# Linear-attention decays computed in another order, and index scores rectified inside PSUM in groups of four

## What is computed

```python
# gla_mixer: chunks of 64 tokens, 4 heads of 256 features
G = jnp.cumsum(g, axis=2)                       # per chunk, in log space
G_last = G[:, :, -1:]
q_t = q * (GLA_DK ** -0.5) * jnp.exp(G)         # decay of the queries
k_t = k * jnp.exp(-G)                           # growth of the keys
k_s = k * jnp.exp(G_last - G)
...                                             # exp(G_last): decay of a whole chunk

# dsa_mixer: 8 index heads of 64, scores of a query against all earlier keys
rel = jax.nn.relu(jnp.einsum('bthd,bsd->bths', qi_b, ki))
score = jnp.einsum('bths,bth->bts', rel, wi_b) * INDEX_SCALE
score = jnp.where(causal[None], score, -jnp.inf)
_, idx = lax.top_k(score, topk)                 # 128 keys for each query
...                                             # softmax attention over those keys
```

## Time and profile before

| | us |
|---|---|
| median of 3 runs | 1694.35 |
| lowest, highest | 1693.36, 1698.34 |
| the profiled execution | 1694.79 |
| its span in the profile | 1693.1 |

### The profile page before, as it was taken

How to read it: one execution, slowest core, us unless ns; L and a number is a source line. 1 busy time by engine, 2 the same in 40 slices (tenths; PEclk the granted TensorE clock), 3 DMA queues, 4 the chain that set the end, 5 groups by cost and what they waited for, 6 DMA issues and landing times. The chain is left out here.

```text
span 1693.1 us, 23540 instructions
## 1 busy us (share of the span) xinstructions
PE 1570.6 (93%) x9993; PEld 1332.1 (79%) x9993; DVE 706.2 (42%) x1357; ACT 526.6 (31%) x849; POOL 590.9 (35%) x245
## 2 busy tenths in 40 slices
PE   6998999999999997999999999999999986957998
PEld 5896885998988974687887997999798763557997
DVE  4031440222162546695555117232242346578524
ACT  2354124333122323234444122352322234331210
POOL 5324320333432256444553242333334460512021
PEclk8999999999999997999999999999999987568999
DMA  5223220134322322122111422342222100020111
GB/s 153 76 75 94 69 62 25 52 99 160 107 95 75 88 85 64 33 93 62 38 51 51 162 76 75 112 146 63 83 92 78 48 1 1 0 75 1 51 51 50
DMA packets 115970, 121.60 MB, mean 72 GB/s; under 512 B 14623, under 2 KB 109833, under 8 KB 115610
## 3 DMA queue, kind: packets, MB, share of 16 engines
q1 hardware_dynamic: 112320, 114.16, 21.3%
q10 hardware_dynamic: 3546, 5.94, 1.0%
HBM read 113.80 MB, written 6.29 MB: 71 GB/s over the span
## 5 line engine op out<-in xcount | busy, mean ns | idle before, releaser
L193 POOL TENSOR_TENSOR w_low<-w_ring,w_high 128x2048 fp32r<-128x2048 f32 (+1 forms) x92 | 419.4, 4559 | 853.0 <-ACT w_high L184 852.9
L209 PE MATMUL ps<-w_high,xT_high 128*128 128x256 f32 (+1 forms) x1056 | 304.5, 288 | 7.8 <-POOL w_low L193 3.4
L209 PE MATMUL ps<-w_high,xT_low 128*128 128x256 f32 (+1 forms) x1056 | 298.9, 283 | 0.0
L209 PE MATMUL ps<-w_low,xT_high 128*128 128x256 f32 (+1 forms) x1056 | 298.8, 283 | 0.0
L184 ACT ACTIVATE w_high<-w_ring 128x2048 fp32r<-128x2048 f32 (+1 forms) x92 | 173.5, 1887 | 355.6 <-PE ps L209 342.2
L209 PE MATMUL ps<-xT_high,w_high 128*128 128x512 f32 (+3 forms) x624 | 253.6, 406 | 8.7 <-DVE mix_a L742 7.7
L209 PE MATMUL ps<-xT_low,w_high 128*128 128x512 f32 (+3 forms) x624 | 249.2, 399 | 0.0
L209 PE MATMUL ps<-xT_high,w_low 128*128 128x512 f32 (+3 forms) x624 | 248.5, 398 | 0.0
L209 PEld LDWEIGHTS ps<-w_high,xT_high 128*128 128x128 f32 x1056 | 202.6, 192 | 15.8 <-issue 10.7
L209 PEld LDWEIGHTS ps<-w_low,xT_high 128*128 128x128 f32 x1056 | 202.6, 192 | 1.7 <-issue 1.7
L209 PEld LDWEIGHTS ps<-w_high,xT_low 128*128 128x128 f32 x1056 | 202.1, 191 | 0.0
(11 more groups left out here) (510 smaller groups left out, 2419.5 us busy)
## 6 DMA issues: line engine op xcount, KB each, us to landing
w_ring<-in_gla_w_in_dram SPq DMA_DIRECT2D x24, 1024.0 KB, 5.4
w_ring<-in_dsa_w_in_dram SPq DMA_DIRECT2D x19, 1024.0 KB, 5.2
w_ring<-in_w_in_dram SPq DMA_DIRECT2D x18, 1024.0 KB, 5.2
w_ring<-in_gla_w_out_dram SPq DMA_DIRECT2D x8, 1024.0 KB, 4.9
w_ring<-in_ple_gate_w_dram SPq DMA_DIRECT2D x8, 1024.0 KB, 5.1
w_ring<-in_dsa_w_out_dram SPq DMA_DIRECT2D x8, 1024.0 KB, 5.3
x_scratch<-x SPq DMA_DIRECT2D x4, 1024.0 KB, 6.6
w_ring<-in_w_out_dram SPq DMA_DIRECT2D x4, 768.0 KB, 4.7
```

The source lines that it names most:

```text
L193: self.nc.gpsimd.tensor_tensor(self.slot(self.w_low, i % RING, k, cols), self.slot(self.w_ring, n % RING, k, cols), self.slot(self.w_high, ...
L209: return self.nc.tensor.matmul(out, lhs, rhs, start=first, stop=last, skip_group_check=not check)
```

## The change

In GLA, ACT's one loop over f becomes three: first the eight small chunk decays, then the eight decays of the queries, then the eight growths of the keys, with the two weight copies before f = 0 and f = 4 of the third loop. The semaphore `decays` becomes three, and DVE waits for the chunk decays before L734, for `q_decay` of tile n before its L742, and for `k_growth` of tile f before its L776.

In DSA, ACT rectifies in place: it reads and writes the PSUM bank, and the buffer `relu` in SBUF is gone. The scores take four banks, m % 4. PE waits for DVE's sum four pairs back; ACT waits for PE only. A projection follows after every fourth pair, six in all (n = 4 to 9), so that ten instead of twelve are left between the scores and the logits.

```diff
                 for f in range(NF):
-                    if f >= 4 and f % 2 == 0:
-                        g.split_high(act, c_q + f // 2 + 1)
                     act.wait_ge(sem["decay_log"], past["decay_log"] + f + 1)
-                    nc.scalar.activation(qT[:, f, :], decay_log[:, f, :], ACT.Exp, scale=1.0 / GATE_NORM).then_inc(sem["decays"], add("decays", 1))
-                    nc.scalar.activation(kT[:, f, :], decay_log[:, f, :], ACT.Exp, scale=-1.0 / GATE_NORM).then_inc(sem["decays"], add("decays", 1))
                     ends = decay_log[:, f, :].rearrange("p (c i) -> p c i", i=C)[:, :, C - 1]
-                    nc.scalar.activation(chunk_decay[:, f, :], ends, ACT.Exp, scale=1.0 / GATE_NORM).then_inc(sem["decays"], add("decays", 1))
+                    nc.scalar.activation(chunk_decay[:, f, :], ends, ACT.Exp, scale=1.0 / GATE_NORM).then_inc(sem["chunk_decay"], add("chunk_decay", 1))
+                for f in range(NF):
+                    nc.scalar.activation(qT[:, f, :], decay_log[:, f, :], ACT.Exp, scale=1.0 / GATE_NORM).then_inc(sem["q_decay"], add("q_decay", 1))
+                for f in range(NF):
+                    if f % 4 == 0:
+                        g.split_high(act, c_q + f // 4 + 3)
+                    nc.scalar.activation(kT[:, f, :], decay_log[:, f, :], ACT.Exp, scale=-1.0 / GATE_NORM).then_inc(sem["k_growth"], add("k_growth", 1))
...
-                dve.wait_ge(sem["decays"], past["decays"] + 3 * NF)
+                dve.wait_ge(sem["chunk_decay"], past["chunk_decay"] + NF)
...
                     dve.wait_ge(sem["qk_ready"], past["qk_ready"] + n + 1)
+                    dve.wait_ge(sem["q_decay"], past["q_decay"] + n + 1)
...
                     dve.wait_ge(sem["qk_ready"], past["qk_ready"] + n + 1)
+                    dve.wait_ge(sem["k_growth"], past["k_growth"] + f + 1)
...
-        relu = probT[:, 0:2]
+        score_bank = lambda m: m % 4
...
-        n_scores = DSA_HEADS // 2
+        n_group = 4
+        n_scores = n_group + 3 * IDX_HEADS // n_group
...
-                    if m >= 2:
-                        pe.wait_ge(sem["relu"], past["relu"] + m - 1)
+                    if m >= 4:
+                        pe.wait_ge(sem["summed"], past["summed"] + m - 3)
...
-                    g.product(ps[:, m % 2, 0:n], qiT[rows, h // 2, j * P:(j + 1) * P], kiT[rows, 0:n]).then_inc(sem["index_ready"], add("index_ready", 1))
-                    if m % 6 == 5 and 4 + m // 6 < n_scores:
-                        project(4 + m // 6)
+                    g.product(ps[:, score_bank(m), 0:n], qiT[rows, h // 2, j * P:(j + 1) * P], kiT[rows, 0:n]).then_inc(sem["index_ready"], add("index_ready", 1))
+                    if m % n_group == n_group - 1:
+                        project(4 + m // n_group)
...
-                    if m >= 2:
-                        act.wait_ge(sem["summed"], past["summed"] + m - 1)
-                    nc.scalar.activation(relu[:, m % 2, 0:n], ps[:, m % 2, 0:n], ACT.Relu).then_inc(sem["relu"], add("relu", 1))
+                    nc.scalar.activation(ps[:, score_bank(m), 0:n], ps[:, score_bank(m), 0:n], ACT.Relu).then_inc(sem["relu"], add("relu", 1))
...
-                    r, w, s = relu[:, m % 2, 0:n], wi[:, j, h:h + 1], score[:, j, 0:n]
+                    r, w, s = ps[:, score_bank(m), 0:n], wi[:, j, h:h + 1], score[:, j, 0:n]
```

More of the change, by code:

```diff
@@ L1345, in logits @@
                         pe.wait_ge(sem["kT_rotated"], past["kT_rotated"] + 1)
-                        pe.wait_ge(sem["relu"], past["relu"] + len(pairs))
+                        pe.wait_ge(sem["summed"], past["summed"] + len(pairs))
                     for j in range(NT):
@@ L1533, in _ @@
                     ins.then_inc(sem["summed"], add("summed", 1))
-                    if m % 6 == 5 and 4 + m // 6 < n_scores:
-                        swap_query(4 + m // 6)
+                    if m % n_group == n_group - 1:
+                        swap_query(4 + m // n_group)
                 dve.wait_ge(sem["summed"], past["summed"] + len(pairs))
```

## The result

The changed kernel takes **1669.49 us** (median of 4 runs, 1666.29 to 1670.68). The kernel before takes 1695.46 us (median of 4 runs, 1693.36 to 1698.34). The ratio is **0.984**, with a 95% interval of 0.983 to 0.986. The prediction was 1669. The profiled execution took 1668.72 us, and its span is 1667.0 us, 26.1 us less than before.

A forecast was written before the change was run, and what follows sets the result against it. PE was taken to bound the kernel, busy 93% of the span, so its waits mattered. 9.1 (GLA) + 19.3 (earlier top-k) - 3 (half clock) = 25.4 us, off 1694.8: forecast 1669, range 1662 to 1677.

The forecast's parts named there:

- GLA, 9.1 us: GLA before query tile 4: PE's 7.73 us idle time goes, plus 1.38 us of slow clock behind it.
- S = 9.5 us: DSA index scores: PE time for six groups of four scores, without their projections, 9.5 us; 17 if pairs did not overlap.
- The start of the top-k, 19.3 us earlier: DSA: DVE's top-k starts at 680.7 instead of 700.01, the most that everything behind it can gain.
- The sums at 0.45 to 0.7 us: DSA scores: DVE's sums, one tensor input in PSUM, take 0.45 to 0.7 us each, as L742 does.
- rival A: DSA scores: sums stay slow beside POOL's splits and DVE paces the groups, 6 us lost, 1675; chance 0.08.
- The rectification in PSUM, taken at 0.6 us: DSA scores: ACT's output into PSUM had no row; 0.6 us assumed, up to 1.2 us costing nothing.
- The new wait, 10.5 us: DSA logits: PE, ahead of DVE's top-k, waits about 10.5 us for the first mask after two free products.
- The half clock behind it, 3 us: DSA logits: PE leaves its new wait at clock 0.50, costing 3 us, between 1.4 and 5 to 6.
- Rival C: DSA logits: half clock lasts longer behind the new wait, 8 us instead of 3, so 1674; chance 0.12.
- The duration of the top-k stays.: DSA: DVE's top-k still takes 66.0 us, its start keeping its distance to PE's projections and POOL's splits.
- Both gains are shifts of everything behind them: GLA and DSA: all later work just moves earlier, PE waiting for no DMA between; 9.1 and 19.3 us.
- The gain of 30.6 us on PE isn't the gain of the kernel: DSA scores: PE needs 31.9 instead of 62.5 us, but the 66.0 us top-k limits what follows to 19.3 us earlier.

The follow-up runs named there:

- The one-wait kernel: New order of GLA's exponentials but one semaphore for all 24, DSA as before, against the kernel before: 1694.25 us, ratio 0.9995.
- the sixes: The changed kernel, still rectifying in PSUM with four banks, but with a projection after every sixth score: 1665.22 us, ratio 0.9816.

## Why the prediction was right, and where its steps were off

- **GLA, 9.1 us: 9.2 in this pair of traces.** The first score is 9.8 us earlier, and 0.55 of that was there before the change begins: POOL's split ahead of the decays starts at 137.38 instead of 137.93. The mechanism held in every trace, with 9.0 to 10.0 us near 404. That all of it reached the first score is luck: in the eight other executions 7.3 to 8.3 us do. The single times held as well: the chunk decays through at 139.6 (said 140.1), `onward` at 142.1 behind POOL's split (said 142.9), L745 at 142.3 (said near 144). "Nothing is late next" held. The one-wait kernel shows that the new order needs the split semaphore.
- **The scores on PE, S = 9.5 us: 10.1.** The groups cost 1.26, 1.68 and 2.11 us instead of 1.15, 1.6 and 2.0. The term that was small is the turn-over of a group, put at 0.3 us: it is 0.4. That the two heads of a pair overlap was right: without that S would have been 17.
- **The start of the top-k, 19.3 us earlier by the DSA part: 18.8** (28.6 - 9.8). The difference is S. The kernel with the DSA part alone gives 63.9 - 45.1 = 18.8 as well.
- **The sums at 0.45 to 0.7 us, held by nothing: 0.48, 0.62 and 0.75** for 256, 384 and 512 columns. The step from L742 with its eight even runs to the sums was right, and with it rival A's chance, though only one of the eight, at 184.87, lay inside a split.
- **The rectification in PSUM, taken at 0.6 us: 0.37, 0.47 and 0.58** by width; into SBUF it was 0.38, 0.49 and 0.60. Doubled, it still cost nothing. The Trainium skill ("ScalarE: Activation LUTs", its tip on the destination in PSUM) has the sign right; what it brings here is 0.01 to 0.02 us a tile.
- **The new wait, 10.5 us: 11.1**, in one piece, before the third logits product, with 0.50 behind it, as said.
- **The half clock behind it, 3 us: 1.9.** From the end of the top-k to the first dense matmul it is 744.93 - 737.44 = 7.5 us, against 771.63 - 766.04 = 5.6 before. The value lay between bounds of 1.4 and 5 to 6, and the lower one, GLA's row, was the nearer. The grant was back before dense work came: 0.50 from 742 to 743, 0.95 in the next us, and the first dense matmul at 744.93. So the thin logits did not hold the half clock, as the upper bound would have had it. Rival C did not happen.
- **The sum.** 9.8 + 18.8 - 1.9 = 26.7 us at the first dense matmul, against 25.4 said. The errors are +0.55 at the start (luck), +0.1, -0.5 and +1.1. Some 0.6 us of it are lost further on, which leaves 26.1 in the span. That the median of 1669.49 meets the 1669 within 0.5 us is in part luck too: single runs of the kernel after spread over 4.4 us, and the kernel before had a median of 1694.35 when the forecast was made and has 1695.46 with its fourth run.

Three things said on the way were weaker than they read.

*"The duration of the top-k stays."* It did, 66.05 us, and the reason given was right: its start keeps its distance to POOL's splits (1.27 us ahead of the next one, before and after). But this is a condition and no property of the top-k. In the kernel that rectifies into SBUF it came 4.3 us later behind the first score and paid 6.9 us for it. So **rival A was mis-sized: some 11 us, not 6** (4.3 + 6.9; the medians differ by 12 to 14, with the 1.7 us of before the first score in it). Its price counted the stretched sums only, and left out that a shifted top-k meets the splits with two operations of its own.

*"Both gains are shifts of everything behind them."* This is true of the two together, and of the DSA part to within 0.5 us in four traces. In the trace of GLA alone 3.8 of 9.4 us were lost in the old stage of the scores, by lower grants behind the same waits, while its medians show the 9.1. And 1.5 us of the GLA part were lost near 400 in eight of nine traces. A shift is whole only while PE gets the same clock in what is shifted, and this the prediction took for granted.

*"The gain of 30.6 us on PE isn't the gain of the kernel"* was right, and it also pointed to the better kernel: DVE's top-k was the limit, not PE, and to begin it between the groups gave 10 us more.

## What to carry to other kernels

Count the gain of a tightened stage by what the slowest engine behind it can start earlier, not by the idle time taken away: here 30 us of PE (62.5 - 22.4 - 10.1) were worth 18.8, because a 66 us chain of DVE stood behind them, and moving a piece of that chain into DVE's pauses brought the next 10. A producer that goes round through two other engines needs as many banks as it issues in a row, and dense work of its own after each row. Two banks more were worth 21.5 us of the kernel here. A group no larger than the banks freed PE for another 11 us, which it then waited for DVE. The change of memory alone was worth nothing measurable with two banks, and some 11 us with four. A new order of results for a waiting engine was worth nothing as long as one semaphore stood for all of them. And measure a stage from a point of its own: the first score alone scattered by 3 us between executions of kernels with the same code ahead of it.

## What the runs showed of the hardware

- A DVE instruction whose tensor inputs all lie in SBUF can be held until POOL's weight split beside it ends: 4.11 us for 128 x 384, 4.06 for 128 x 128, 2.46 for a copy of 128 x 32. The max and replace instructions of the top-k were not held (0.43 and 0.41 us for 128 x 256). With one of two inputs in PSUM and a weight column in SBUF as scalar an instruction took 0.48, 0.62 or 0.75 us by width beside the same splits. I had taken this from eight rows of L742; that the price would also appear in the top-k I had not expected.
- The granted clock also fell behind waits shorter than the longest of the earlier trace rows. With waits of 2.28, 0.52, 2.02 and 0.59 us, each inside a group of thin 64-row products, the dense projections behind them ran at 0.74 and 0.80. With waits of up to 2.7 us and two banks it was 0.65 to 0.70. Without any wait the same thin products kept it at 1.00 over 44 us. Half of a stage's loss can so lie where PE looks fully busy: of the 11.5 us that the sixes cost more than the fours, the waits are 5.4.
- The same wait didn't always bring the same grant. Behind a wait of 2.23 us near 400, the same kernel had 1.00 in one execution and 0.66 in another (400 to 405). Behind waits of 0.47, 0.3 and 0.29 us the same projection had 1.00 in one kernel and 0.68 in another. With single traces a difference of 1 to 4 us can be this alone.
